# A two-block transformer step: the first weight block by quarters, one transpose for two norms, and weight splits and norms in another order

## The reference, cut to what matters

```python
# first block
h = rms_norm(x, norm1_g);  proj = h @ w_in            # q, ckv, qi, ki, wi, u, v, ga, gb
... sparse attention, gated MLP, merge, x = x + merged @ w_out
h2 = rms_norm(x, norm2_g);  x = x + hier_moe(h2)      # 1 of 4 groups, 2 of its 8 experts
x = rms_norm(x, final_norm_g)
# second block: two layers
x = x + dilated_mixer(rmsnorm(x, a_norm), a_w_in, a_w_out)
x = x + swiglu(rmsnorm(x, ffn_norm[0]), ffn_w_gu[0], ffn_w_down[0])
x = x + forgetting_mixer(rmsnorm(x, b_norm), b_w_in, b_f, b_w_out)
x = x + swiglu(rmsnorm(x, ffn_norm[1]), ffn_w_gu[1], ffn_w_down[1])
out = rmsnorm(x, final_norm)
```

## Time and profile before

| what | us |
|---|---|
| median of 3 runs (2580.19 to 2588.78) | 2581.22 |
| the profiled execution | 2584.21 |
| its span, first to last instruction | 2582.4 |
| PE busy in matmuls | 2472.3 (96%) |
| DVE busy | 975.2 (38%) |
| ACT busy | 963.9 (37%) |
| POOL busy | 920.4 (36%) |

### The profile page before, as it was taken

How to read it: one execution, slowest core, us unless ns; L and a number is a source line. 1 busy time by engine, 2 the same in 40 slices (tenths; PEclk the granted TensorE clock), 3 DMA queues, 4 the chain that set the end, 5 groups by cost and what they waited for, 6 DMA issues and landing times.

```text
span 2582.4 us, 31198 instructions
## 1 busy us (share of the span) xinstructions
PE 2472.3 (96%) x11684; PEld 1943.6 (75%) x11684; DVE 975.2 (38%) x1622; ACT 963.9 (37%) x1594; POOL 920.4 (36%) x772
## 2 busy tenths in 40 slices
PE   6999999999995999999999999999899999999998
PEld 5766687555545998899987788888687777788886
DVE  3166445878874233363334521111201113311112
ACT  3234433656653233343343432222333333422213
POOL 4332132424332333333332244545431221444444
PEclk9999999999997999999999999999999999999999
DMA  5412026899973222312222123232221111223232
GB/s 161 157 58 66 33 98 259 302 389 394 381 277 130 82 82 86 96 66 67 98 82 67 50 81 98 86 99 84 91 83 66 66 49 33 82 98 98 98 89 82
DMA packets 209228, 314.06 MB, mean 122 GB/s; under 512 B 19888, under 2 KB 139312, under 8 KB 199392
## 3 DMA queue, kind: packets, MB, share of 16 engines
q1 hardware_dynamic: 201408, 299.79, 33.6%
q0 software_dynamic: 7712, 12.76, 1.5%
HBM read 300.81 MB, written 22.71 MB: 125 GB/s over the span
## 4 chain that ended last, share of the span: by engine, by line
PE 44%; issue 34%; POOL 17%; DMA 2%; DVE 1%; ACT 1%; SPq 0%; POOLq 0%; DVEq 0%; ACTq 0%
POOL w_low L2851 17%; PE bank L820 9%; PE bank L822 8%; PE bank L821 8%; PE bank L1230 4%; PE bank L1209 2%; PE bank L1214 2%; PE bank L1371 2%; PE bank L1393 2%; DMA w_ring<-in_w_gate 2%; PE bank L859 1%; PE bank L1026 1%; PE bank L1380 1%; PE bank L960 1%; PE bank L1191 1%
## 5 line engine op out<-in xcount | busy, mean ns | idle before, releaser
L2851 POOL TENSOR_TENSOR w_low<-raw,w_high 128x512 fp32r<-128x512 f32 x592 | 776.1, 1343 | 1382.6 <-ACT w_high L1612 1382.6
L820 PE MATMUL bank<-h_high,w_high 128*128 128x512 f32 x1088 | 438.9, 403 | 10.8 <-DVE h_low L2136 7.6
L822 PE MATMUL bank<-h_high,w_low 128*128 128x512 f32 x1088 | 427.7, 393 | 0.0
L821 PE MATMUL bank<-h_low,w_high 128*128 128x512 f32 x1088 | 427.3, 393 | 0.0
L1612 ACT ACTIVATE w_high<-raw 128x2048 fp32r<-128x2048 f32 x149 | 284.3, 1909 | 306.2 <-PE bank L822 301.6
L820 PE MATMUL bank<-w_high,h_high 128*128 128x512 f32 (+2 forms) x832 | 332.3, 399 | 14.3 <-POOL w_low L2851 10.8
L822 PE MATMUL bank<-w_high,h_low 128*128 128x512 f32 (+2 forms) x832 | 311.8, 375 | 0.0
L821 PE MATMUL bank<-w_low,h_high 128*128 128x512 f32 (+2 forms) x832 | 311.6, 375 | 0.0
L820 PEld LDWEIGHTS bank<-h_high,w_high 128*128 128x128 f32 x1088 | 206.6, 190 | 68.2 <-issue 13.3
L822 PEld LDWEIGHTS bank<-h_high,w_low 128*128 128x128 f32 x1088 | 206.2, 190 | 44.3
L821 PEld LDWEIGHTS bank<-h_low,w_high 128*128 128x128 f32 x1088 | 206.9, 190 | 39.0
(11 more groups left out here) (344 smaller groups left out, 3485.3 us busy)
## 6 DMA issues: line engine op xcount, KB each, us to landing
raw<-in_ffn_w_gu SPq DMA_DIRECT2D x88, 512.0 KB, 4.4
raw<-in_a_w_in SPq DMA_DIRECT2D x72, 512.0 KB, 4.6
w_ring<-in_w_gate SPq DMA_DIRECT2D x35, 1024.0 KB, 8.8
w_ring<-in_w_up SPq DMA_DIRECT2D x35, 1024.0 KB, 10.9
w_ring<-in_w_down SPq DMA_DIRECT2D x35, 1024.0 KB, 7.5
raw<-in_ffn_w_down SPq DMA_DIRECT2D x40, 512.0 KB, 4.2
raw<-in_w_in SPq DMA_DIRECT2D x34, 512.0 KB, 4.4
raw<-in_b_w_in SPq DMA_DIRECT2D x24, 512.0 KB, 4.7
```

What stands on the lines that cost most here:

```text
L820: pe.matmul(out, sta[0], mov[0], start=start, stop=False)
L821: pe.matmul(out, sta[0], mov[1], start=False, stop=False)
L822: return pe.matmul(out, sta[1], mov[0], start=False, stop=stop)
L2851: last = pool.tensor_tensor(out=w_low[:, slot, cols], in0=raw[:, slot, cols], in1=w_high[:, slot, cols].bitcast(F32), op=ALU.subtract)
```

## The change

- **Front.** The identity alone (64 KB) is loaded ahead of block 0, the rest of the table behind it, `w_spatial` behind block 1. Block 0's high half is made by ACT in quarters, in turn with the first four turned chunks, and POOL follows by quarters, each counted on its own; PE's product of chunk k waits for quarter k // 2. Block 1's high half comes after chunk 3. The transposes of `w_spatial` come after the products. One more gain column joins the small DMAs.
- **Border.** PE, ACT and DVE no longer wait for each other at phases 6 and 7. X is turned as it is, unscaled; the column factor is the product of both gains (`gg`). DVE scales X into xn, a tile ahead of each of the first four low halves, ACT takes the squares of xn for the second norm, and the product of both row factors (`r12`) is multiplied in when ACT empties the projection, in all six rounds of it. A round trip through DRAM (`d_r`) gives the row factors in the strided order. A DMA copies xn back to X. The first projection takes four tiles a chunk (`first_four`), more PSUM banks, and both pairs of tiles with one block before the next.
- **Order.** Ahead of the first feed-forward the last norm tile's square comes before ACT's last weight copy. A round of a feed-forward starts when two of the four last adds are done. In the last round DVE makes two low halves in place of POOL, and the second half of the outputs takes its short block first. The forget columns are loaded and split in the feed-forward.

```diff
-        sp.dma_start(cst[:, :], a["table"]).then_inc(cst_loaded, 16)
-        sp.dma_start(ws_raw[:, :, :], a["w_spatial"][0].rearrange("g i j -> i g j")).then_inc(ws_loaded, 16)
+        sp.dma_start(cst[:, 0:P], a["table"][:, 0:P]).then_inc(ident_loaded, 16)
...
+        sp.dma_start(cst[:, P:C_COLS], a["table"][:, P:C_COLS]).then_inc(cst_loaded, 16)
         load_tall(B_Q, w_in, 0)
+        sp.dma_start(ws_raw[:, :, :], a["w_spatial"][0].rearrange("g i j -> i g j")).then_inc(ws_loaded, 16)
...
+                    if v == 0 and kind == 1 and kh == 0:
+                        sp.wait_ge(nm_rows, 4 * NT)
+                        sp.dma_start(d_r.rearrange("(t p) -> p t", p=P), r12[:, 0, :],
+                                     allow_slow_non_contiguous=True).then_inc(row_moved, 16)
+                        sp.wait_ge(row_moved, 16)
+                        sp.dma_start(r12[:, 1, :], d_r.rearrange("(p t) -> p t", t=NT)).then_inc(row_moved, 16)
+                    if v == 0 and kind == 2 and kh == 0:
+                        sp.wait_ge(dl_out, NT)
+                        sp.dma_start(X[:, :, :], xn[:, :, :]).then_inc(x_again, 16)
...
-        phase_end(6)
-        pe.wait_ge(nm_rows, 2 * NT + 5)
-        keep_clock(4)
-        phase_end(7)
         phase_mark()
+        pe.wait_ge(y_summed, 2)
+        keep_clock(3)
+        pe.wait_ge(y_summed, NT)
...
-        turn_norm(3, first_two)
+        first = chunk[0]
+        for c in range(KD + 2):
+            if c >= 2:
+                pe.wait_ge(turn_free, first + c - 1)
+                first_four(c - 2)
+            if c < KD:
+                turn([X[:, t, c * P:(c + 1) * P] for t in range(NT)])
...
+                        if r:
+                            pe.wait_ge(ff_down_free, down0 - 2)
...
-        split_high(0, 0, 1)
+        act.wait_ge(raw_loaded[0], 32)
         act.wait_ge(gcol_loaded, 16)
+        for c in range(KD):
+            if c < 4:
+                cols = slice(512 * c, 512 * c + 512)
+                act.activation(w_high[:, 0, cols], raw[:, 0, cols], ACT.Copy).then_inc(q_high if c < 3 else high_done, 1)
+            turned_high(h_high[:, c, :], gcol[:, 0, c:c + 1])
+            if c == 3:
+                split_high(1, 1, 1)
...
-        act.wait_ge(vec_loaded, 16 * 7)
+        act.wait_ge(vec_loaded, 16 * 8)
...
-            turned_high(h_high[:, c, :], gcol[:, 2, c:c + 1])
-            if c == 1:
+            turned_high(h_high[:, c, :], gg[:, c:c + 1])
+            if c < NT:
+                second_squares(c)
+            if c == 0:
                 split_high(B_DIL + 1, (B_DIL + 1) % 2, (B_DIL + 1) // 2 + 1)
...
-                act.activation(dst, G[2 + t % 2][:, :], ACT.Copy).then_inc(dl_evac, 1)
+                act.activation(dst, bank_of(v, kind, t)[:, :], ACT.Copy, scale=r12[:, order_of(v), t:t + 1])\
+                   .then_inc(dl_evac, 1)
...
+                        if r == 2 and half == 0 and t in (0, NT - 1):
+                            n = B_FFN[l] + FF_BLOCK[2] + 8 + t // (NT - 1)
+                            dve.wait_ge(high_done, n + 1)
+                            sub(w_low[:, n % 2, :], raw[:, n % 2, :], w_high[:, n % 2, :].bitcast(F32)).then_inc(low_done, 1)
...
-        for n in range(2):
-            split_low(n, n)
+        for q in range(4):
+            pool.wait_ge(q_high if q < 3 else high_done, q + 1 if q < 3 else 1)
+            cols = slice(512 * q, 512 * q + 512)
+            pool.tensor_tensor(out=w_low[:, 0, cols], in0=raw[:, 0, cols], in1=w_high[:, 0, cols].bitcast(F32),
+                               op=ALU.subtract).then_inc(q_low if q < 3 else low_done, 1)
+        split_low(1, 1)
         for i in range(1, 6):
             column(i).then_inc(vec_loaded, 16)
+        column(6).then_inc(vec_loaded, 16)
```

More of the change, by code:

```diff
@@ L107, in small @@
         return t
-    gcol = small("gcol", [P, 6, KD])
+    gcol = small("gcol", [P, 7, KD])
+    gg = small("gg", [P, KD])
+    r12 = small("r12", [P, 2, NT])
+    rstd2 = small("rstd2", [P, NT])
     ones_col = small("ones_col", [P, 1])
@@ L536, in out_group, with ffn_part @@
         return OUT_LAST[g - 16] + (6, 2)
+    def ffn_part(r, half, i):
+        part = 1 - i if r == 2 and half else i
+        return 4 * part, min(4, FF_ROUNDS[r] - 4 * part)
     def tokens(t, chunk, tile, order):
@@ L762, in ffn_loads @@
                         n = n0 + chunks + 2 * half + i
-                        k0, kn = FF_CHUNK[r] + 4 * i, min(4, chunks - 4 * i)
+                        k0, kn = ffn_part(r, half, i)
+                        k0 += FF_CHUNK[r]
                         dst = shaped(raw, n % 2, 4)
@@ L886, in by_rows @@
                 last.then_inc(block_used, 1)
-        pe.wait_ge(cst_loaded, 16)
-        pe.wait_ge(ws_loaded, 16)
-        turn([ws_raw[:, g, :] for g in range(4)])
+        pe.wait_ge(ident_loaded, 16)
         hh = (h_high, h_low)
@@ L929, in _ @@
         turn_norm(0, misc_product)
+        pe.wait_ge(cst_loaded, 16)
+        pe.wait_ge(ws_loaded, 16)
+        turn([ws_raw[:, g, :] for g in range(4)])
         def bias_row(h):
@@ L1312, in first_two @@
             wh, wl = weights((B_DIL + c // 4) % 2, 4)
-            for t in range(2):
-                last = pass3(G[2 + t][:, :], [tokens(x, c, t, order_of(0)) for x in hh],
+            for t in range(NT):
+                last = pass3(bank_of(0, 0, t)[:, :], [tokens(x, c, t, order_of(0)) for x in hh],
                              (wh[:, c % 4, :], wl[:, c % 4, :]), c == 0, c == KD - 1)
@@ L1938, in after_group @@
                 ahead(B_AOUT + (0 if what[0] == "first" else 2) + what[1])
-        for i in range(1, 12):
+        act.wait_ge(row_moved, 32)
+        for i in range(2, 12):
             empty_pair(0, i)
@@ L2039, in _ @@
         phase_end(11)
-        act.wait_ge(fo_loaded, 32)
-        act.activation(fw_split[:, :, 0:16], fw_raw[:, :, :], ACT.Copy).then_inc(fo_high, 1)
         turned_norm(4)
@@ L2180, in _ @@
             norm_tile(t, t, xn)
+        dve.wait_ge(gcol_loaded, 16)
+        for c in range(KD):
+            turned_low(h_low[:, c, :], h_high[:, c, :], gcol[:, 0, c:c + 1])
         dve.wait_ge(cst_loaded, 16)
@@ L2188, in _ @@
             cst[:, C_TRI:C_TRI + P].unsqueeze(1).broadcast_to([P, 4, P])).then_inc(turn_free, 1)
-        for c in range(KD):
-            turned_low(h_low[:, c, :], h_high[:, c, :], gcol[:, 0, c:c + 1])
         dve.wait_ge(band_vec_loaded, 32)
@@ L2585, in _ @@
             dve.tensor_copy(xg[:, b, 0:1], G[2][0:R, 0:1])
-        phase_end(6)
-        dve.wait_ge(gw1_loaded, 16)
-        def combine(t):
+        phase_mark()
+        dve.wait_ge(gains_loaded, 32)
+        mul(gg[:, :], gcol[:, NORM_A, :], gcol[:, 6, :])
+        for t in range(NT):
             dve.wait_ge(tile_loaded[t], 48)
@@ L2760, in _ @@
             if AO_FILL[f] == ("tile", NT - 1):
-                for t in range(NT - 1):
+                for t in range(NT - 2):
                     norm_tile(NT * 4 + t, t, xn)
-        norm_tile(NT * 4 + NT - 1, NT - 1, xn)
+        for t in range(NT - 2, NT):
+            norm_tile(NT * 4 + t, t, xn)
         phase_mark()
```

163 lines of the change are left out of this document (97 added, 66 removed).

## The result

The changed kernel takes 2550.3 us (median of 4, 2549.4 to 2550.5) beside 2583.6 for the kernel before in the same rounds: ratio 0.987, 95% interval 0.985 to 0.989. Forecast were 2552.6 and a gain of 28.6; the gain in the same rounds is 33.3. The profiled execution took 2550.2 (span 2548.3) beside 2584.2 (span 2582.4), 34.1 less by the spans.

The account below looks back on a forecast made before the run. TensorE, busy 96% of the span, was taken as the bound, so only its waits and half-rate time could be won. Terms summed to -28.6 us: 2555.6 profiled, 2552.6 for the median, range 2543 to 2564.

Parts of the forecast that it names:

- Front: Start of kernel: first product 7.7 us sooner, but later waits and half rate leave net +0.4 us, bounds -6.0 and +2.3.
- about 2.1 us are lost to half rate: Front, behind PE's 5.6 us idle at the second bias row: the clock falls until 4.1 us of work restore it.
- Border: Between the two blocks: first product 10.8 us sooner, POOL stalls gone, some costs; sum -12.3 us, bounds -14.8 and -8.
- the even chance: Between the blocks: the clock is as likely as not to be lost around the transposes, counted as 1.1 us.
- the price of 2.2: Between the blocks: 2.2 us lost if the clock falls around the transposes.
- 0.9 + 0.5 + 1.1: Between the blocks, costs in us: next block's split on ACT, DVE's extra scaling beside POOL, possible loss of clock.
- the 4.0 for the stalls: First dilated projection: PE's four waits for POOL's low halves go, worth 4.0 us.
- Done by 818: Row factors' DRAM round trip: starts near 808, done by 818 at the latest, needed from 821, so hidden.
- they lie beside PE: 0: The 72 evacuations with a row factor may take 0.69 instead of 0.60 us; no cost, at worst +6.5.
- Rival C: Between 798 and 803, DVE's norm scalings and POOL's low quarters exclude each other: about 1.5 us more, 2554; chance 0.10.
- Into the first feed-forward, feed-forwards, fox, tail: Stages behind the border: shorter waits and queues, clock kept at norms; -2.2, -6.4, -6.4 and -1.7 us.
- granted clock 1.00 all through: Sign to look for in the forgetting attention: the clock stays full; not losing it was counted as -1.8 us.

Follow-up runs that it names:

- e3: Changed kernel with five dummy matmuls of PE ahead of the second bias row; 2547.6 us, ratio 0.988.
- e9: Changed kernel with DVE copying the first bias row's bands out before the key normalisation, nothing else; 2543.7 us, ratio 0.986.
- e1: Changed kernel with the front of the kernel before, border and order parts kept; 2549.3 us, ratio 0.988.
- e7: Changed kernel with the store of the row factors done twice before they are loaded back; 2562.1 us, ratio 0.993.
- e8: Changed kernel with first projections' banks copied out without the second norm's row factor and the wait for it (result lacks it); 2548.1 us, ratio 0.988.
- e5: Kernel before with the new front and nothing else; 2582.2 us, ratio 1.0002.
- e4: Kernel before with only the order edits behind the border; 2563.7 us, ratio 0.993.
- e6: Changed kernel with ACT's small-column wait behind the first two projections and first bias row's bands copied before the key normalisation; 2544.9 us, ratio 0.986.
- e10: Changed kernel with the old front and the first bias row's bands copied out before the key normalisation; 2546.9 us, ratio 0.986.
- e11: Changed kernel, unaltered, timed again; 2553.0 us, ratio 0.989.
- e2: Changed kernel with ACT's wait for the small columns moved behind the q and index projections; 2547.3 us, ratio 0.987.

## Why the prediction came out right

The places and the mechanisms of the gain were right, the sizes less so. The time was 2.3 us from the forecast, but the gain was 33.3 in the same rounds and 34.1 between the two traces, where 28.6 was forecast. That the time came closer is luck: the sum was taken from a median of 2581.2, and the same kernel took 2583.6 in the rounds of the comparison. By terms the traces give +2.1 for the front (forecast +0.4), +2.7 for the experts (0), -16.4 for the border (-12.3) and -22.5 for the rest (-16.7), of which 3.4 are the single loss in the profiled execution of before.

**Front** (forecast +0.4, measured +2.1). The chain is the one described: ids wait, ACT, four key scalings beside POOL, bands; PE's wait was 4.9 (5.6 forecast) and its end 45.33 (45.1). Two misses cancelled in it: ids were issued at 34.41, 1.4 later than the sum has them, and landed 3.0 later and not 4.1. Mis-sized is the term "about 2.1 us are lost to half rate": it was 3.9, since PE ran 7.8 us at half rate before the clock was back and not 4.1 as in the row I took it from. e3 and e9 confirm both halves: without the clock's fall 3.1 less, without the wait 8.5 less. What e9 adds is that the wait goes with the columns as late as before, once two small copies have another place in DVE's order; the prediction took that order as given.

**Border** (forecast -12.3, measured -17.8 as -11.9 and -5.9; the +1.3 of "dilated" is the factor's, below). The place and mechanism were right, every size on the careful side, so that the sum passed its own bound of -14.8. First product 11.9 sooner (10.9 to 11.1 in four runs) where 10.8 was forecast. The clock stayed up behind the turns in eight of the eleven profiles with the new border; in e1, e7 and e9 it fell (0.50 at 792 to 794 in e9), and the projection stage of e1 and e9 is 1.2 longer. Three in eleven do not refute the even chance; the price of 2.2 was too high. The four POOL stalls went, and each had cost more than its length. From start to start the products follow at 0.23 to 0.24 in the stream; over the four stalls of before it is 1.84, 0.90, 1.86 and 0.90, and the first product after each takes 0.46 to 0.47 before the next can start. So four stalls of 3.9 were worth 5.5 (4.0 in the sum), and the tile order of before had further such stops in its last chunks, worth 0.8. The 0.9 for the weight copy between chunks 0 and 1 came out as 0.3, and of the 0.5 for DVE beside POOL nothing shows. The step that failed most in size is the costs' side, "0.9 + 0.5 + 1.1", where 0.3 came, and next to it the 4.0 for the stalls.

**Row factors.** "Done by 818" was wrong, "hidden" right: the store of 2 KB took 8.1 us to its signal (9.5 in e7), outside the 1.6 to 4.1 of the earlier trace rows, and the load was issued at 820.09. Evacuations "they lie beside PE: 0" was wrong in kind: they turned up as 1.3 us of PE's time, as e8 shows, by way of the weight blocks behind them; the prediction had named this as a sign against it, with 6.5 as its bound. The copy back of X (issued 826.04, landed in 8.4) was hidden.

**Rival C** (DVE's norm scaling and POOL exclude each other) came true as a mechanism and not as a price. DVE and POOL in the changed kernel:

```profile
799.39 1.28 DVE L2681 SCALAR_TENSOR_TENSOR xn<-X,rstd,gw 128x1024 f32<-128x1024 f32 x1
...
803.13 2.23 DVE L2681 SCALAR_TENSOR_TENSOR xn<-X,rstd,gw 128x1024 f32<-128x1024 f32 x1
```

```profile
801.76 7.01 POOL L2939 TENSOR_TENSOR w_low<-raw,w_high 128x512 fp32r<-128x512 f32 x4 [22.32 <-ACT w_high L1672]
816.09 5.02 POOL L2939 TENSOR_TENSOR w_low<-raw,w_high 128x512 fp32r<-128x512 f32 x4 [7.32 <-ACT w_high L1672]
```

The first scaling that meets POOL takes 0.95 us longer, the next (1.47 at 806.14) 0.19, POOL's four quarters 2.0 longer, and PE waits for neither. The Trainium skill, page "SBUF — State Buffer", section "Who interferes with whom", says that a DVE instruction with two SBUF inputs contends with a GpSimd instruction that reads SBUF; by that rule, the trace agrees. Whether PE then waits is read from the trace alone.

**Into the first feed-forward, feed-forwards, fox, tail** (forecast -2.2, -6.4, -6.4, -1.7; together -16.7). Against e5: 16.5 in e4, 19.7 in the profile after. Within it, by the same products of after and before set side by side, the norm into the first feed-forward gave 2.7 and 0.6 right behind it, 3.3 in all; the clock stayed (the forecast had an even chance), and the first product now waits 1.70 for POOL's low half, where it had waited 1.17 for DVE. Each wait of 0.78 gave 1.1 and each of 1.66 gave 1.95: again some 0.3 more than the stop's length. So the feed-forwards gave 8.3, where the sum has the bare lengths of the waits, 6.4, as its bound too. At the fox entry the traces give 6.1. The tail gave 1.69. The sign "granted clock 1.00 all through" did not come: fox has 10.2 us at half rate from 1851.9 and 3.4 from 2094.3, as before had from 1877.3 and 2187.9, neither of them at the norm.

**Not foreseen**: the expert stage, given nothing, took 2.7 us more in the profile after, 0.4 ahead of the loop and 2.3 in the loop, where PE waits 6.9 us in nine pieces for ACT before its down products, and 5.0 in seven pieces in before. In the eleven profiles with the new border the loop takes +0.6 (e6, e7) to +3.2 (e10), in the three without it -0.2 (e4), 0 (before) and +0.7 (e5). So an effect of the change on the loop is neither shown nor excluded; what makes it was not tried.

## What to carry to other kernels

A stage that starts sooner only helps until the next wait that another engine ends: before shortening a load, follow the second and third wait behind it, and look at what that engine does *first* in its own order. Here a 7 us earlier start was worth nothing, and moving two copies of 0.9 us together made it worth 4.5 to 5.1 at the marker. Count a removed stall with its restart (0.3 to 0.4 us here beyond the stall's length) and with the clock behind it, and judge edits of this size by stages of the trace, not by the whole time.

## What the runs showed of the hardware

- The same code keeps the full clock over a 1.1 us pause in one execution (before, e1) and loses it in another (e4, 0.50 in 50 to 52). After the 4.9 us pause it was lost in all four profiles that have it (after, e7, e8, e11), and after the one of 2.6 us in e2. At half rate, PE worked 7.8 us before the clock was back in after, and 3.4 in e4.
- A store of one float per partition and column to DRAM (2 KB) took 8.1 us from issue to its signal, in e7 9.5; the load of the same 2 KB took 3.5, and the copy of 2 MB from SBUF to SBUF 8.4.
- A DVE operation of 0.29 us on 128x128 took 3.62 when it met POOL's quarters (e2), nearly three of POOL's own operations of 1.27.
- A bank's copy on ACT with a scale per row takes 0.69 instead of 0.60 (e8).
